# mLSTM stages of a hybrid decoder step: gate rows projected between the last query chunks, row-maxima broadcasts one chunk later, decode value sums at the last chunk of a pass

## What is computed

```python
(mq, mk, mv, mo, mi, mf, cb, cc, cx, sq, sk, sv, gates) = jnp.split(xn @ w_in, split_points, axis=-1)
i_pre = (mi + b_if[:M_HEADS]).astype(f32)
log_f = jax.nn.log_sigmoid((mf + b_if[M_HEADS:]).astype(f32))
hm, C, n, m = mlstm_chunkwise(mq, mk, mv, i_pre, log_f, C0, n0, m0)   # running row maxima of b[t]-b[s]+i[s]
ym = jax.nn.sigmoid(mo) * hm
# decode attention: z = q.k/sqrt(d) + b_sb over the cached pages,
# a = exp(log_sigmoid(z) + sum of log_sigmoid(-z) over later keys), out = a @ v
```

## Time and profile before

| | us |
|---|---|
| median of 3 runs | 2130.42 (2129.45 to 2134.44) |
| the profiled execution's own time | 2130.93 |
| its span, first to last instruction | 2129.2 |
| PE busy in the span | 2055.4 (97%) |
| DVE, POOL, ACT busy | 886.3, 634.2, 436.6 |
| mean granted TensorE clock | 0.981 |

### The profile page before, as it was taken

The page is one execution under the profiler, slowest core; times in us unless marked ns, Lnnn a source line. Parts: engine busy times, 40 slices in busy tenths (PEclk is TensorE's granted clock), DMA queues, the critical chain, the costliest instruction groups (busy, mean ns, idle before and its releaser), DMA issues. The chain is left out here.

```text
span 2129.2 us, 34700 instructions
## 1 busy us (share of the span) xinstructions
PE 2055.4 (97%) x12957; PEld 1999.0 (94%) x12957; DVE 886.3 (42%) x1455; ACT 436.6 (21%) x843; POOL 634.2 (30%) x417
## 2 busy tenths in 40 slices
PE   7999999999999899999989999999999999999997
PEld 6999999988988899988889999999999999999997
DVE  4111444452556466543448443313411421344457
ACT  4112333321111122222123122101200200221212
POOL 5233223221322122212234232332332333233434
PEclk9999999999999899999899999999999999999999
DMA  7331212233442455535456211111111111111313
GB/s 191 89 80 41 55 50 60 60 99 87 138 126 75 127 168 143 152 105 164 115 169 198 61 41 50 49 41 50 49 40 49 49 42 46 49 49 40 99 50 130
DMA packets 244682, 185.08 MB, mean 87 GB/s; under 512 B 15206, under 2 KB 218034, under 8 KB 244340
## 3 DMA queue, kind: packets, MB, share of 16 engines
q1 hardware_dynamic: 235476, 165.96, 27.3%
q10 hardware_dynamic: 9120, 17.93, 2.3%
HBM read 150.82 MB, written 33.06 MB: 86 GB/s over the span
## 5 line engine op out<-in xcount | busy, mean ns | idle before, releaser
L143 PE MATMUL acc<-x_hi,w_hi 128*128 128x344 f32 x2496 | 818.7, 328 | 21.8 <-PEq L1091 5.1
L143 PE MATMUL acc<-x_lo,w_hi 128*128 128x344 f32 x2496 | 804.4, 322 | 0.0
L143 PE MATMUL acc<-x_hi,w_lo 128*128 128x344 f32 x2496 | 804.3, 322 | 0.0
L113 POOL TENSOR_SCALAR w_hi<-w_raw 128x1024 fp32r<-128x1024 f32 (+1 forms) x176 | 182.4, 1036 | 1281.3 <-PE acc L143 1072.1
L143 PEld LDWEIGHTS acc<-x_hi,w_hi 128*128 128x128 f32 x2496 | 476.0, 191 | 31.5 <-issue 17.2
L143 PEld LDWEIGHTS acc<-x_lo,w_hi 128*128 128x128 f32 x2496 | 475.7, 191 | 1.9 <-issue 1.9
L143 PEld LDWEIGHTS acc<-x_hi,w_lo 128*128 128x128 f32 x2496 | 475.4, 190 | 0.0
L116 POOL TENSOR_TENSOR w_lo<-w_raw,w_hi 128x1024 fp32r<-128x1024 f32 (+1 forms) x176 | 406.3, 2308 | 14.7
L143 PE MATMUL acc<-z_hi,w_hi 128*128 128x344 f32 x768 | 245.9, 320 | 0.0
L143 PE MATMUL acc<-z_hi,w_lo 128*128 128x344 f32 x768 | 245.3, 319 | 0.0
L143 PE MATMUL acc<-z_lo,w_hi 128*128 128x344 f32 x768 | 245.1, 319 | 0.0
(11 more groups left out here) (304 smaller groups left out, 2105.1 us busy)
## 6 DMA issues: line engine op xcount, KB each, us to landing
w_raw<-in_w_in SPq DMA_DIRECT2D x64, 512.0 KB, 4.3
page<-in_cache_k SPq DMA_DIRECT2D x64, 256.0 KB, 2.8
v_page<-in_cache_v SPq DMA_DIRECT2D x64, 256.0 KB, 2.7
w_raw<-in_w_up SPq DMA_DIRECT2D x32, 512.0 KB, 4.0
w_raw<-in_w_down SPq DMA_DIRECT2D x32, 512.0 KB, 3.9
merge_gate<-merge_gates SPq DMA_DIRECT2D x22, 516.0 KB, 3.9
merge_gates<-gate_out ACTq DMA_DIRECT2D x16, 516.0 KB, 3.3
w_raw<-in_w_ple_gate SPq DMA_DIRECT2D x16, 512.0 KB, 4.1
```

The costliest lines, as they stand in the source:

```text
L113: nc.gpsimd.tensor_scalar(k.w_hi[:, par, 0:kb, :], k.w_raw[:, par, 0:kb, :], 1.0, 1.0, ALU.mult, ALU.mult).then_inc(k.w_rounded, 1)
L143: mm = k.nc.tensor.matmul(k.acc[:, c, 0:CW], w[:, par, i, :], x[:, i, cols], start=(i == 0 and j == 0), stop=(i == kb - 1 and j == 2))
```

## The change

Five edits, all in the order of instructions. The gate rows of a chunk are projected right after the same chunk of the last query block, on PE and on ACT, and the query group is written out instead of looped. The 18 small matmuls move from behind MQ to behind MK. The broadcasts of row maxima move from chunks 0 and 2 to chunks 1 and 2 (at chunk 1 of every other block behind the query row's broadcast). The sum for the decode weights moves from behind the last chunk of GATES to before it. The decode value sums move from before slot 3 to before slot 5, and wait for the copy of slot 3's bank in place of slot 0's.

```diff
@@ -832,26 +832,35 @@
                             pe.wait_ge(s["multiplied"], q * PAGES + RING)
                             nc.tensor.matmul(q_row[:, :], k.ones[0:B, :], q_own[:, :], start=True, stop=True)\
                                 .then_inc(s["rows_ready"], 1)
-                        if gi == MO and c != 1:
-                            t = b * 2 + c // 2
+                        if gi == MO and c:
+                            t = b * 2 + c - 1
                             pe.wait_ge(s["spread_ready"], t + 1)
                             pe.wait_ge(s["g_rows_read"], t + 1)
-                            nc.tensor.matmul(g_rows[:, c // 2, :], k.ones[:, :], spread[:, c // 2, :, :],
+                            nc.tensor.matmul(g_rows[:, c - 1, :], k.ones[:, :], spread[:, c - 1, :, :],
                                              start=True, stop=True).then_inc(s["g_rows_ready"], 1)
+                        if gi == MQ and b == H - 1:
+                            project_gates(c)
+                        if gi == GATES and b == LATE_GATES - 1 and c == 1:
+                            pe.wait_ge(s["sp_ready"], 1)
+                            nc.tensor.matmul(sums[:, 0:N], k.neg_from[:, :], sp_[:, :, :, :].rearrange(flat), start=True, stop=False)
+                            nc.tensor.matmul(sums[:, 0:N], k.neg_ones[:, :], later[:, :, :, :].rearrange(flat),
+                                             start=False, stop=True).then_inc(s["z_summed"], 1)
+
+                def project_gates(c):
+                    cols = slice(c * CW, (c + 1) * CW)
+                    if c:
+                        pe.wait_ge(s["if_read"], c)
+                    else:
+                        pe.wait_ge(s["w_ready"], 1)
+                    for i in range(KD):
+                        nc.tensor.matmul(by_gate[:, 0:CW], w_if2[:, i, :, :], k.x_hi[:, i, cols],
+                                         start=(i == 0), stop=False, skip_group_check=True)
+                        mm = nc.tensor.matmul(by_gate[0:2 * H, 0:CW], w_if2[:, i, 0, :], k.x_lo[:, i, cols],
+                                              start=False, stop=(i == KD - 1), skip_group_check=True)
+                    mm.then_inc(s["if_ready"], 1)
 
                 def after(gi):
-                    if gi == MQ:
-                        pe.wait_ge(s["w_ready"], 1)
-                        for c in range(NCH):
-                            cols = slice(c * CW, (c + 1) * CW)
-                            if c:
-                                pe.wait_ge(s["if_read"], c)
-                            for i in range(KD):
-                                nc.tensor.matmul(by_gate[:, 0:CW], w_if2[:, i, :, :], k.x_hi[:, i, cols],
-                                                 start=(i == 0), stop=False, skip_group_check=True)
-                                mm = nc.tensor.matmul(by_gate[0:2 * H, 0:CW], w_if2[:, i, 0, :], k.x_lo[:, i, cols],
-                                                      start=False, stop=(i == KD - 1), skip_group_check=True)
-                            mm.then_inc(s["if_ready"], 1)
+                    if gi == MK:
                         pe.wait_ge(s["if_read"], NCH)
                         for tb in range(TB + 1):
                             m = P if tb < TB else B
@@ -864,13 +873,8 @@
                         nc.tensor.matmul(sums[:, 0:GATE_COLS], k.sum_to[:, :], lf, start=True, stop=True)
                         nc.tensor.matmul(sums[:, GATE_COLS:2 * GATE_COLS], k.ones[:, :], lf, start=True, stop=True)\
                             .then_inc(s["summed"], 1)
-                    if gi == GATES:
-                        pe.wait_ge(s["sp_ready"], 1)
-                        nc.tensor.matmul(sums[:, 0:N], k.neg_from[:, :], sp_[:, :, :, :].rearrange(flat), start=True, stop=False)
-                        nc.tensor.matmul(sums[:, 0:N], k.neg_ones[:, :], later[:, :, :, :].rearrange(flat),
-                                         start=False, stop=True).then_inc(s["z_summed"], 1)
-
-                walk(pe, step, after)
+
+                walk(pe, step, after, straight=(MQ,))
 
             @block.scalar
             def _(act):
@@ -886,6 +890,10 @@
                         acc_wait(k, act, n, c)
                         nc.scalar.activation(out[:, :, c * CW:(c + 1) * CW], k.acc[:, c:c + 1, 0:CW],
                                              g["func"], scale=g["scale"]).then_inc(k.acc_free, 1)
+                        if gi == MQ and b == H - 1:
+                            act.wait_ge(s["if_ready"], c + 1)
+                            nc.scalar.activation(if_rows[:, c * CW:(c + 1) * CW], by_gate[:, 0:CW], ACT.Copy)\
+                              .then_inc(s["if_read"], 1)
                     if to_dram:
                         act.wait_ge(k.acc_free, (n + 1) * NCH + NCH)
                         act.dma_start(k.gates[:, b + FIRST_GATE:b + FIRST_GATE + 1, :], out).then_inc(gate_sent[par], 16)
@@ -899,11 +907,6 @@
                     return op
 
                 def after(gi):
-                    if gi == MQ:
-                        for c in range(NCH):
-                            act.wait_ge(s["if_ready"], c + 1)
-                            nc.scalar.activation(if_rows[:, c * CW:(c + 1) * CW], by_gate[:, 0:CW], ACT.Copy)\
-                              .then_inc(s["if_read"], 1)
                     if gi == MK:
                         act.preload_act_table_set(EXP_LN)
                         act.wait_ge(s["raw_ready"], 1)
@@ -918,7 +921,7 @@
                         act.wait_ge(s["arg_ready"], 1)
                         nc.scalar.activation(k.dec_prob[:, :, :, :].rearrange(flat), z_abs[:, :, :, :].rearrange(flat), ACT.Exp)
 
-                walk(act, step, after)
+                walk(act, step, after, straight=(MQ,))
                 for par in range(2):
                     act.wait_ge(gate_sent[par], LATE_GATES // 2 * 16 + 16)
 
@@ -1167,7 +1170,7 @@
 
                 def sum_values(c):
                     pe.wait_ge(s["weighed"], (c + 1) * PAGES)
-                    pe.wait_ge(k.acc_free, (base + c * NB + 1) * NCH + 1)
+                    pe.wait_ge(k.acc_free, (base + c * NB + 2) * NCH + 1)
                     for h in range(H):
                         mm = nc.tensor.matmul(y[:, bass.ds(c, 1), h], v_sum[:, h, :], k.ones[:, 0:1], start=True, stop=True)
                     mm.then_inc(s["dec_summed"], 1)
@@ -1175,7 +1178,7 @@
                 with pe.Fori(0, TB) as c:
                     for slot in range(SLOTS):
                         b, ch = divmod(slot, NCH)
-                        if slot == NCH:
+                        if slot == SLOTS - 1:
                             sum_values(c)
                         project_chunk(k, pe, base + c * NB + b, b, ch, k.x_hi, k.x_lo)
                         if slot == 0:
```

## The result

The changed kernel takes 2112.46 us (median of 4 runs, 2111.04 to 2118.53) against 2130.45 us for the kernel before on the same chip; the ratio is 0.9918, 95% interval 0.9905 to 0.9931. That is 18.0 us less, and 2113 was predicted. The profiled execution is the slowest of the four: 2118.53 us, span 2116.8, only 12.4 us less than the profiled execution before. Stretches of it can be compared; its total says less than the median does.

The account below looks back on a forecast made before the run. TensorE, at work in 97% of the span, was taken to bound the kernel. Terms 2.1 + 1.7 + 6.8 - 0.9 + 8.25 = 18.0 us came off 2130.93, giving 2113, range 2107 to 2121.

Parts of the forecast that it names:

- Gate rows, 2.1 us of waits: Gate rows between query chunks: TensorE's three waits for ACT's copy, 0.69 us each, become hidden; 2.1 us gained.
- Clock behind the small matmuls, 1.7 us taken as gained: Behind the 18 small matmuls: the clock's fall to 0.79 over 8 us goes; 1.7 us gained, bounds 0 and 1.7.
- The sum, 18.0 us: Whole kernel: 2.1 + 1.7 + 6.8 - 0.9 + 8.25 = 18.0 us less, giving 2113.
- Row maxima, 6.8 us: Broadcasts of row maxima one chunk later: four waits for `g_spread` go; 6.8 us gained, bounds 5.7 and 6.8.
- The margin of ACT behind them: GATES: ACT's copy of the first gate chunk stays in time, margin about 1 us becoming about 0.7; cost 0, at worst 0.5.
- The weight sum costs 0.9 us: End of GATES: sums before the last chunk delay its DMA; cost 0.9 us, bounds a cost of 0.9 and gain of 0.3.
- Value sums, 8.25 us: First pass: wait of 5.59 us for DVE's eighth page and low clock behind it go; gain 8.25 us, lower bound 3.6.
- `h_tok` comes late: Rival, first pass: TensorE waits 1 to 3 us for `h_tok`, total 2115 to 2119; chance 12%.
- one of the signs of being wrong: Profile after: wait for `h_tok` in pass one, for `acc_free` in GATES, or clock below 1.00 between 490 and 520 us.
- my margin of 0.5 us: First pass: DVE has `h_tok` at 732.85, TensorE would ask at 733.3, so it is there 0.5 us early.
- The clock falls elsewhere: Rival, whole kernel: the shift makes one fall more or fewer, or keeps that behind the small matmuls; 2109 to 2117, 14%.
- 5.5 us of margin: GATES: DVE's chain for the weight sum ends 13.3 us after the stage's start, asked for at 18.8 us; no wait.

Follow-up runs that it names:

- e1: Kernel before with only the gate-row edits (gate rows between last query chunks, 18 small matmuls behind MK): 2131.68 us, ratio 0.9997.
- e7: Changed kernel with the gate rows put back behind the query group: 2114.86 us, 0.9925 of before.
- e5: Changed kernel with the decode weights' sum put back behind the last chunk: 2113.56 us, 0.9912 of before.
- e8: Changed kernel run again with no edit: 2111.16 us, 0.9906 of before.
- e12: Changed kernel without a store behind the last gate chunk, that block's place getting the block before: 2112.59 us, one run.
- e11: Changed kernel with the 18 small matmuls done twice in a row, same output: 2114.18 us, one run.
- e3: Kernel before with only the decode weights' sum moved before the last gate chunk: 2132.18 us, ratio 1.0008.
- e4: Kernel before with only the decode value sums moved, before slot 5 in place of slot 3: 2123.49 us, ratio 0.9964.
- e2: Kernel before with only the broadcasts of row maxima one chunk later: 2124.91 us, ratio 0.9964.
- e10: Changed kernel with the 18 small matmuls spread, six behind each of three chunks of MK's last block: 2110.85 us, 0.9905 of before.

## Why the prediction was right, point by point

*Gate rows, 2.1 us of waits.* Measured 2.04 (A in e1 and in the changed kernel; back in e7). Right.

*Clock behind the small matmuls, 1.7 us taken as gained.* This step was wrong. I held the wait of 0.54 us in front of them needed for the fall, and took one wait of 2.44 us with full clock behind it as a sign that idle time so short does nothing. Of five traces with 18 in one piece and no wait in front (changed, e1, e5, e8, e12) four have the fall; all five with the wait have it; none of three with the pieces spread has it. The wait made it a little surer at most; the small matmuls in one piece bring it, and e11 doubles its cost. With the fall A is 82.95, in e8 without it 81.40, so it costs 1.55 us. And of the eight waits of 2.4 us for `g_spread` in before, e1, e3 and e4, two have a fall behind them: a single place with full clock showed too little.

*The sum, 18.0 us.* Here luck helped. The traces account for 16.5 us from A to D2, and the prediction without its 1.7 us is 16.3. The agreement of 2112.46 with 2113 needs some 1.5 us more, which no trace gives to the change: the profiled execution has 1.3 us ahead of A, where the instructions are the same, and then loses more than that in E. Executions of one kernel differ by 7 to 9 us (changed, e8), more than any small term of the sum.

*Row maxima, 6.8 us.* Measured 6.73. Right. The margin of ACT behind them was predicted to shrink from 1 to 0.7 us: ACT began to copy the first gate chunk 678.66 - 668.33 = 10.3 us after the start of GATES, 10.1 before, of 11.3 that TensorE allows; the copy itself takes 0.4 us of what is left. No wait. Timeline of ACT in the changed kernel, to set beside the earlier trace rows:

```profile
678.66 0.79 ACT L891 ACTIVATE mp_gate_out<-acc 128x344 f32<-128x344 f32 x2
...
692.95 0.34 ACTq L899 DMA_DIRECT2D merge_gates<-mp_gate_out  x1
693.33 0.42 ACT L922 ACTIVATE dec_prob<-dec_z_abs 128x256 f32<-128x256 f32 x1 [0.41 <-ACT mp_gate_out L891]
```

*The weight sum costs 0.9 us.* Measured 0.91 (e3, changed) and 0.90 (e5) in the trace; no total shows it clear of noise. The store issued at 692.95 moved behind the sums with the last chunk; e12 shows that it ends the stage, and the exponential, done at 693.75, does not.

*Value sums, 8.25 us.* Measured 8.41 alone, and D1 and D2 together 8.66 less in the changed kernel. The rival "`h_tok` comes late" holds in part, and the wait of 0.66 us is one of the signs of being wrong that I had named: my margin of 0.5 us was too large. In e4, with a D1 of 6.6 us, `h_tok` is done at 731.55 and TensorE takes it at 731.75, so 0.2 us; with a shorter D1 nothing is left. DVE has `h_tok` 25.7 to 27.1 us after the stage's start in these traces, however TensorE comes through D1, so most of what TensorE gains in D1 below 5.8 us it waits for again: D1 spans 3.9 to 6.6 us, and D1 and D2 together stay at 34.9 to 36.4 us in all ten traces with the late sums.

*The clock falls elsewhere.* This rival is part of what separates executions of one kernel: e8 against the first profile. Its range, 2109 to 2117, holds the forecast too, so the total can't tell the two apart. The Trainium skill ("TensorE: Matmul & The Clock Gate", Part 1) calls the activity window free-running; two traces of the changed kernel fit that (0.86 and 1.00 for the same instructions), but no run here isolates the phase.

*Not foreseen:* E varies between 205.2 and 212.2 us. In seven traces (changed, e1, e2, e4, e5, e8, e12) TensorE waits once more for `w_lo` late in it, 1.9 to 2.6 us, and E is 209.7 us or more; in the other seven that wait is 0.3 us at most and E 208.5 us or less. The change alone doesn't decide it: e7, e10 and e11 are free of it, e2 and e4, with one part each, are not. What does stays open.

## What to carry to other kernels

A wait for a copy between two uses of one bank can cost nothing once a chunk of independent matmuls stands between them, as it did here (3.8 us of matmuls against a loss of 0.7 us); look for such a chunk before adding a buffer. Before moving work ahead of the last chunk of a stage, ask what ends the stage: here it is the store behind that chunk, so everything put ahead of it is paid in full. When an engine is paced by another from the start of a stage, speed gained ahead of the meeting point comes back as a wait. And before trusting a total that agrees to 1 us, cut the traces at the same instructions: here a wrong term and a lucky one hid each other.

## What the runs showed of the hardware that was not expected

Eighteen matmuls of 8 columns, 2.0 us in which PE counts as busy, let the clock fall to 1.2 GHz behind them in four of five traces; in three pieces of six, with a chunk of dense matmuls between them, in none of three.

Seven additions of 32 columns on DVE (L1024 before, L1027 after) took 2.47 us before and 4.78 us after. The changed kernel's timeline of DVE, and the last two of the seven by themselves (windows 680.62:681.65 and 681.7:684.2):

```profile
679.33 4.78 DVE L1027 TENSOR_TENSOR dec_later<-dec_later,dec_sp 128x32 f32<-128x32 f32 x7
...
680.66 0.95 DVE L1027 TENSOR_TENSOR dec_later<-dec_later,dec_sp 128x32 f32<-128x32 f32 x1
...
681.69 2.42 DVE L1027 TENSOR_TENSOR dec_later<-dec_later,dec_sp 128x32 f32<-128x32 f32 x1
```

POOL in the same stretch:

```profile
680.52 1.06 POOL L113 TENSOR_SCALAR w_hi<-w_raw 128x1024 fp32r<-128x1024 f32 x1 [8.65 <-PE acc L143]
681.66 2.40 POOL L116 TENSOR_TENSOR w_lo<-w_raw,w_hi 128x1024 fp32r<-128x1024 f32 x1
```

The first five additions take 0.19 us each. The sixth starts while POOL makes `w_hi` and ends with it (681.61 and 681.58 us), the seventh starts while POOL makes `w_lo` and ends with that (684.11 and 684.06 us). So DVE is not slowed in proportion: one small addition is held for as long as POOL's instruction lasts. The 14 traces agree: in the ten in which the seventh addition meets `w_lo` it takes 2.42 us, in the four in which it meets `w_hi` (before, e1, e3, e4; POOL starts at 690.61 us in before) 0.87 or 0.88 us. The chain was ready at 684.1, 3.5 us before TensorE asked at 687.62; 5.5 us of margin had been predicted. It fits the Trainium skill ("GPSIMD Engine Reference", Specifications), which names contention for DVE instructions with two SBUF inputs, as these additions have; no run here changes POOL's work alone.

The same thing lengthens the first pass. In the kernel before, the four products of one page take 4.17 us where a page that meets no instruction of POOL takes 1.14:

```profile
723.27 4.17 DVE L1258 SCALAR_TENSOR_TENSOR v_sum<-v_page,dec_prob,v_sum 128x128 f32<-128x128 f32 x4 [0.23 <-issue]
727.67 1.14 DVE L1258 SCALAR_TENSOR_TENSOR v_sum<-v_page,dec_prob,v_sum 128x128 f32<-128x128 f32 x4 [0.23 <-issue]
```

These 3 us are part of what TensorE waited for there (5.59 us). What moving POOL's work would give was not tried.
